# Three rounds of an expert choice set between gathered rows, and GpSimd's requests for rows set between its parts of these rounds

## The reference, cut to what matters

```python
def one_block(xb):                       # 128 tokens
    q = (xb @ w_q).reshape(n, 8, 256); q1, q2 = split(q)
    s1 = einsum('nhd,hkd->nhk', q1, sub_k1); s2 = ...        # 128 keys each
    v1, i1 = top_k(s1, 16); v2, i2 = top_k(s2, 16)
    cand = (v1[..., :, None] + v2[..., None, :]).reshape(n, 8, 256)
    top_s, top_c = top_k(cand, 16)
    idx = take(i1, top_c // 16) * 128 + take(i2, top_c % 16)
    act = gelu(einsum('nhkd,nd->nhk', e_down[idx], xb))
    return einsum('nhk,nhkd->nd', softmax(top_s) * act, e_up[idx])
```

## Time and profile before

| | us |
|---|---|
| median of 3 runs (lowest to highest) | 2693.71 (2691.06 to 2698.30) |
| the profiled execution | 2692.59 |
| its span, first to last instruction | 2690.8 |
| busy: PE 2439.7, PEld 2116.3, DVE 2208.6, ACT 1107.1, POOL 1339.9 | 91%, 79%, 82%, 41%, 50% of the span |

### The profile page before, as it was taken

One profiled execution on the slowest core, in us unless ns is written; L12 is line 12 of the kernel. 1 busy time (PEld: TensorE's weight loads), 2 busy tenths in 40 slices (PEclk: granted clock), 3 DMA queues, 4 the chain that ended last, 5 costly groups with the idle time before them and its releaser, 6 DMA issues.

```text
span 2690.8 us, 38692 instructions
## 1 busy us (share of the span) xinstructions
PE 2439.7 (91%) x13259; PEld 2116.3 (79%) x13259; DVE 2208.6 (82%) x3961; ACT 1107.1 (41%) x1938; POOL 1339.9 (50%) x1054
## 2 busy tenths in 40 slices
PE   7989999899988999999825669999999999999998
PEld 5767889788866788778614668999999999989997
DVE  6355546986688888865799979999999999999998
ACT  4453544333266223333217983333333333343333
POOL 0000000326613445634454447787777777767874
PEclk9999999999999999999867899999999999999999
DMA  6735547458954878968802359999999999999996
GB/s 240 276 119 206 182 165 289 154 195 312 365 160 149 305 285 312 349 250 339 351 0 91 161 212 416 399 414 415 415 404 400 403 398 409 404 394 386 415 413 248
DMA packets 237396, 793.77 MB, mean 295 GB/s; under 512 B 21568, under 2 KB 70768, under 8 KB 214992
## 3 DMA queue, kind: packets, MB, share of 16 engines
q0 software_dynamic: 112288, 408.77, 39.0%
q1 hardware_dynamic: 124976, 383.29, 37.9%
HBM read 731.16 MB, written 60.82 MB: 294 GB/s over the span
## 4 chain that ended last, share of the span: by engine, by line
PE 64%; DVE 19%; DMA 8%; ACT 4%; issue 3%; POOL 1%; SPq 0%; POOLq 0%; DVEq 0%; ACTq 0%
PE lin L242 14%; PE lin L243 13%; PE lin L244 13%; PE tr L242 6%; PE tr L243 6%; PE tr L244 6%; DMA row_ring<-in_down,IDX 4%; DVE w_lo L219 2%; DMA w_raw<-in_wall 2%; DVE row_ring L136 2%; DVE w_hi L1902 2%; ACT w_hi L211 1%; DVE mark L1907 1%; DVE att_nmx L1104 1%; POOL row_ring L148 1%
## 5 line engine op out<-in xcount | busy, mean ns | idle before, releaser
L148 POOL DMA_INDIRECT row_ring<-in_down,IDX x256 | 339.8, 1327 | 367.1 <-DVE dots L136 299.2
L242 PE MATMUL lin<-w_hi,T_hi 128*128 128x512 f32 x976 | 392.8, 402 | 15.0 <-DVE w_lo L219 7.0
L243 PE MATMUL lin<-w_lo,T_hi 128*128 128x512 f32 x976 | 388.8, 398 | 0.0
L219 DVE TENSOR_TENSOR w_lo<-w_raw,w_hi 128x2048 fp32r<-128x2048 f32 x94 | 216.4, 2302 | 210.0 <-ACT w_hi L211 205.9
L244 PE MATMUL lin<-w_hi,T_lo 128*128 128x512 f32 x976 | 388.5, 398 | 0.0
L136 DVE CUSTOM_DVE_ANT_0 row_ring<-row_ring,H 128x1024 f32<-128x1024 f32 x256 | 304.7, 1221 | 84.4 <-DMA row_ring<-in_down,IDX 83.0
L211 ACT ACTIVATE w_hi<-w_raw 128x2048 fp32r<-128x2048 f32 x116 | 222.0, 1914 | 368.3 <-PE lin L244 327.3
L242 PE MATMUL tr<-T_hi,w_hi 128*128 128x384 f32 x1024 | 349.3, 341 | 3.1 <-DVE w_lo L2204 3.1
L244 PE MATMUL tr<-T_hi,w_lo 128*128 128x384 f32 x1024 | 346.2, 338 | 0.0
L243 PE MATMUL tr<-T_lo,w_hi 128*128 128x384 f32 x1024 | 345.8, 338 | 0.0
L2114 POOL DMA_INDIRECT rows<-in_up,now x192 | 305.1, 1589 | 77.5 <-issue 53.0
(11 more groups left out here) (291 smaller groups left out, 5259.5 us busy)
## 6 DMA issues: line engine op xcount, KB each, us to landing
w_raw<-in_wall SPq DMA_DIRECT2D x116, 1024.0 KB
G<-in_downT SPq DMA_DIRECT2D x128, 512.0 KB
row_ring<-in_up SPq DMA_DIRECT2D x128, 512.0 KB
wd<-dense_gates SPq DMA_DIRECT2D x32, 768.0 KB
weight_rests<-w_lo SPq DMA_DIRECT2D x22, 1024.0 KB, 4.8
w_lo<-weight_rests SPq DMA_DIRECT2D x22, 1024.0 KB
dense_gates<-peer SPq DMA_DIRECT2D x6, 2048.0 KB, 6.5
dense_gates<-w_raw SPq DMA_DIRECT2D x6, 2048.0 KB, 6.9
```

What stands on the lines that cost most here:

```text
L148: pool.indirect_dma_start(self.ring[:, r % self.K, :], None, self.table, bass.IndirectOffsetOnAxis(ap=self.IDX[:, r:r + 1], axis=0)).then_ ...
L219: dve.tensor_tensor(self.lo[:, h % 2], self.raw[:, h % 2], self.hi[:, h % 2].bitcast(F32), ALU.subtract).then_inc(self.lo_done, 1)
L242: pe.matmul(out, lhs[0], rhs[0], start=start, stop=False, skip_group_check=True)
L243: pe.matmul(out, lhs[0], rhs[1], start=False, stop=False, skip_group_check=True)
```

## The change

On VectorE: 8 rows instead of 5 ahead of each chunk of the output projection, 14 rows (instead of 12, and then all the rest) ahead of round 0, one row at each `aside()` of rounds 0 to 2, and the rows that are left behind round 2. The calls of `st.split_lo` that go had no effect. On GpSimd: rows are asked up to six beyond the 33 rows that VectorE takes ahead of round 0. Then come 4 rows ahead of each of rounds 0 to 2, 1 row between its additions and its look-up, 1 row behind each look-up, and all that are left ahead of round 3. Nothing is computed otherwise than before.

```diff
+        EARLY, ROWS_XO, ROWS_FIRST = 3, 8, 14
             for c in range(2):
-                bg.dve(dve, 5)
+                bg.dve(dve, ROWS_XO)
                 st.split_lo(dve, H0 + 2 * c + 2)
...
+            def one_row():
+                bg.dve(dve, 1)
...
-            bg.dve(dve, 6)
-            st.split_lo(dve, H0 + 6)
-            bg.dve(dve, 6)
-            st.split_lo(dve, H0 + 7)
+            bg.dve(dve, ROWS_FIRST)
+            assert all(st.is_loaded(H0 + h) for h in range(6, 12))
+            for r in range(EARLY):
+                pick_experts(r, one_row)
             bg.finish(dve)
-            for c in range(1, NPC):
-                pick_experts(2 * c - 2)
-                if c < NPC - 1:
-                    st.split_lo(dve, H0 + 6 + 2 * c)
-                pick_experts(2 * c - 1)
-                if c < NPC - 1:
-                    st.split_lo(dve, H0 + 7 + 2 * c)
-            pick_experts(6)
-            pick_experts(7)
+            for r in range(EARLY, 8):
+                pick_experts(r)
...
-            bg.pool(pool, bg.end)
+            taken = begun + 2 * ROWS_XO + NT - 1 + ROWS_FIRST
+            def more_rows(n):
+                nonlocal taken
+                taken += n
+                bg.pool(pool, min(taken + bg.K, bg.end))
+            more_rows(0)
             for r in range(UNITS + 1):
                 u = r
+                if r == EARLY:
+                    bg.pool(pool, bg.end)
                 if u < UNITS:
+                    if r < EARLY:
+                        more_rows(4)
                     pool.wait_ge(halved, u + 1)
...                  # pairs added (L1967), ids copied (L1971)
+                    if r < EARLY:
+                        more_rows(1)
                 u = r - 1
                 if u >= 0:
                     pool.wait_ge(marked, u + 1)
...                  # ids looked up (L1978, L1983, L1989)
+                    if r < EARLY:
+                        more_rows(1)
```

More of the change, by code:

```diff
@@ L1559, in routing_and_gates @@
         place = m.sb("place", [P, TOPK, LOOK], BF16)
+        begun = bg.done
         score_rows = [G[:].rearrange("p t (u j k) -> p (t u) j k", u=2, j=4),
```

## The result

The changed kernel takes 2679.46 us (median of 6 runs, 2674.39 to 2684.39) beside 2692.39 (6 runs) of the kernel before. The ratio is 0.995, with a 95% interval of 0.9937 to 0.9963, so 0.5% faster, about 13 us. The profiled execution took 2679.31, with a span of 2677.5 against 2690.8. Forecast were 2681.0 and 2679.9. (One execution of the later kernel xo_only, 3560.64 us, was in the chip's slower state and stands outside its ratio.)

What follows compares the result with a forecast made beforehand. The stage was taken as bound by DMA until 1335, then by VectorE. The steps put round 3 at 1349.9 instead of 1362.6, 12.7 us sooner: 2679.9 profiled, 2681.0 from the median, range 2669 to 2691.

Steps and rivals of the forecast that it cites:

- TensorE held at chunk 1: Output projection: 8 rows ahead of chunk 0's additions delay the first addition, so TensorE waits about 2.7 us.
- last row ahead of chunk 1 landed: Output projection: the last of 8 rows, requested shortly before a weight load, lands at 1234 (bounds 1229.5 to 1236).
- first row behind the norm: VectorE after the projection: transposes come some 6 us later, so this row starts at 1252.6 instead of 1246.6.
- 14 rows: VectorE ahead of round 0: these keep their old pattern and take 26.1 us, ending at 1278.7.
- rounds 0 to 2, with all waits in front of and in them: VectorE: rounds with 17 rows between their parts, 43.8 us of work plus 2.5 waits and 2.6 holds, ending at 1327.9.
- the last 13 rows: VectorE behind round 2: a late request behind the look-up makes them take 19 to 25 us, middle 22.
- the two landing waits: Start of the rounds, with the ring empty: VectorE waits for rows 15 and 16, 1.4 + 1.1 = 2.5 us.
- The holds: Rounds 0 to 2: GpSimd's additions and look-up and VectorE's rows delay each other, 2.6 us in all (bounds 0 and 6).
- Rival (a): Rows ahead of the chunks land in time or the last 13 flow as before: 23 us gained, 2670; chance 0.23.
- (b): Rows between rounds cost more, as the ring runs low in each round: 3 us of gain, 2691; chance 0.21.
- (c): GpSimd's requests fall into step with the rounds, the ring empties in each: 6 us slower, 2700; chance 0.06.
- Rival (d): Round 0 waits for its scores anyway and the rounds stay behind the rows; chance 0.02.

Runs made afterwards that it cites:

- xo_only: Changed kernel with only its added rows ahead of the projection's chunks, all rounds behind the last row as before; ratio 0.9997 to the kernel before.
- last_lookup: Changed kernel, but GpSimd makes unit 1's look-up only after VectorE has used the last row; ratio 0.9928 to the kernel before.
- late_lookup: Changed kernel, but GpSimd makes unit 1's look-up only after asking for the last 13 rows; ratio 0.9939 to the kernel before.
- the block: Changed kernel with rounds 0 to 2 in one piece behind the 14 rows, no rows or requests between their parts; ratio 1.0009 to the kernel before.
- last_again: The same kernel as last_lookup, run and profiled a second time; ratio 0.993 to the kernel before.
- both_last: last_lookup with unit 0's look-up also moved behind the last row; ratio 0.9928 to the kernel before.
- xo58_last: last_lookup with 5 rows ahead of chunk 0 of the projection and 8 ahead of chunk 1; ratio 0.9923 to the kernel before.

## Why the prediction was right

| step | forecast | measured |
|---|---|---|
| TensorE held at chunk 1 | 2.7 | 2.75 |
| last row ahead of chunk 1 landed | 1234 | by 1231.9 |
| first row behind the norm | 1252.6 | 1250.3 |
| 14 rows | 26.1 | 25.9 |
| rounds 0 to 2, with all waits in front of and in them | 49.2 | 47.5 |
| the last 13 rows | 22 (19 to 25) | 25.4 |
| round 3 starts | 1349.9 | 1349.1 |
| from round 3 to the end | unchanged | 0.1 longer |

The sum was right to 0.8 us, but two of its terms were not, and their errors cancelled. The start came 2.3 us sooner than forecast and the rounds were 1.7 us shorter, while the last rows took 3.4 us longer. That the sum hit so closely is luck. The first 14 rows alone took between 24.8 and 28.8 us in the profiles of kernels whose code up to there is the same. What the experiments bear out is the mechanism: rounds in VectorE's waits for rows, and a gain of the size of half of the 24.2 us moved.

The hit on TensorE's hold is luck too. The forecast let TensorE need the addition at 1212.6 and VectorE begin it at 1214.6. In the changed kernel TensorE was ready at 1210.9 (1213.64 less 2.75) and VectorE began at 1212.8. Chunk 0 went faster there, since TensorE's granted clock was 1.00 from 1188 to 1196, where the profile of before has 0.74 and 0.84. And the eighth row was used at 1211.7, where it had landed at 1213.4. Both errors are 1.7 to 1.8 us and cancel.

The landing ahead of chunk 1 was sized by a request that met a load of weights 1.5 us later. The step left out that the load is itself tied to TensorE. ScalarE's rounding of the half before it waits for TensorE. It began at 1226.7 instead of 1223.8, so the load came at 1229.0 instead of 1226.1, and the row, asked for at 1223.65, was there by 1231.9. With that TensorE stood idle for 1.79 us ahead of the transposes, not the 4 to 5 forecast, and kept its clock. That this landing can also come later was inside the bound (1236). One profile of last_lookup had 1237.

Within the rounds the two landing waits are there, 1.09 and 2.44 us (1.4 and 1.1 forecast). The holds were over-charged. Three rows took 1.64, 1.79 and 1.36 us instead of 1.22, 1.1 in all instead of 2.6. GpSimd's additions were the ones to be held, with 1.52 us for the pair of them in round 0 where 0.71 is usual.

For the last rows the forecast took the middle of two bounds, where the pessimistic one, 25, came to 0.4 us of what was measured. Its parts did not: the next request came 8.3 us after round 2 (9 forecast) and its row landed 4.4 us later (5.5), but the seven rows behind it took 11.6 us instead of 8.8. Every step of the look-up met a row. Rows 12 had shown the pattern, a look-up step and a two-operand instruction in turn. There was no reason to expect back-to-back rows to escape it half the time. late_lookup and last_lookup take this term apart. Without the late requests the 13 rows take 3.9 us less. The holds at the end are 3.2 us, of which 1.7 to 2.4 us came back in the last rows once they were gone, the rest going into landing waits.

The Trainium skill (SBUF — State Buffer, Who interferes with whom) gives the taking of turns as a rule, and this trace agrees with 2.93 us for a row of 1.22 beside GpSimd's step of 2.06. Its inference that requests for DMA are not touched by such instructions stays open here. Requests beside back-to-back rows took 1.69, 1.98 and 1.99 us at 1251.7 to 1256.0 of the changed kernel, and mostly 0.94 in the last rows of last_lookup, with one of 1.68 at 1330.5. I had read the first kind as speaking against the page, and the second kind does not.

Rival (a), 23 us, was wrong in the kernel as it stands. The part of it that foretold a gain if the last rows flowed as before is what last_lookup brings (19.8 us for the last 13 rows, 18 in the rival). Rivals (b) and (c) did not come: the ring did not run low in each round. Rival (d), scores that come too late, cost 0.5 us here, and in the block 11.3.

The best kernels run here are those with the look-up behind the last row, last_lookup, last_again, both_last and xo58_last, with medians of 2671.3 to 2671.7 us and ratios of 0.992 to 0.993. They are faster than the changed kernel by another 0.2 to 0.3%. Each interval overlaps that of the changed kernel slightly, but the four medians agree within 0.4 us.

## What to carry to other kernels

Where one engine waits for transfers and a chain of the same engine stands behind them, put the chain between the transfers piece by piece and not in a block. A small ring covers only a few microseconds (here six rows of 1.25 us), and the rounds in one block left the DMA engines at 0.08 to 0.6. Then look at the engine that issues the transfers: what it computes ahead of its next request is paid in late landings, here about 4 us for a look-up that nobody needed for another 20. Before moving more, work out which third engine waits for the last transfer; its cover was 7 us, and one round more used it up. Last, read the same kernel's profile twice before believing a difference between two profiles: here one kernel differed by 3.3 us from itself.

## What the runs showed of the hardware

A VectorE dot product over two SBUF operands and a GpSimd tensor instruction held one another for whole instructions: 1.22 us became 2.93, 2.17, 1.68 and 1.44 beside steps that take 1.9, 1.2, 0.7 and 0.4 alone, and GpSimd's three additions of 2.4 us took 5.0. VectorE's MAX8, with one operand, was not lengthened by a look-up beside it (0.87 for four, as always). So these two engines meet at more than semaphores.

In front of 32 transposes TensorE's clock stayed at 1.00 after idle stretches of 1.0 to 2.65 us, and they took 3.71 us. After 3.36 us they took 5.16 (granted clock 0.71 from 1244 to 1248 in xo58_last). After 4.68, 6.49 and 7.87 us they took 6.38, 5.62 and 6.66, with a granted clock of 0.50. So beyond some length the idle time alone does not order them.
